# One 1.5 MB fetch per weight chunk in place of a 1 MB and a 0.5 MB fetch, in a two-layer decoder trunk

## The chip, the cores and the metric

The kernel runs on one core of a Trainium2 chip. The metric is the device time in microseconds; lower is better. Five engines work beside each other: TensorE (PE; its weight loads are PEld), VectorE (DVE), ScalarE (ACT), GpSimd (POOL) and SyncE (SP), which here issues nearly all DMAs. Each engine works through its own instructions in order, and they wait for each other on semaphores.

## The reference, cut to what matters

Two layers, each an FFN, a mixing block and a second FFN, on 256 tokens of width 1024 in float32:

```python
for l in range(DEPTH):            # DEPTH = 2
    h = h + 0.5 * swiglu(rms_norm(h, ffn1_norm[l]), ffn1_gate[l], ffn1_up[l], ffn1_down[l])
    h = h + token_mixing(rms_norm(h, mix_norm[l]), w_in[l], ...)   # top-k sparse attention beside a forgetting attention
    h = h + 0.5 * swiglu(rms_norm(h, ffn2_norm[l]), ffn2_gate[l], ffn2_up[l], ffn2_down[l])
return rms_norm(h, final_norm)
```

`swiglu` has an inner width of 2816, which is 22 tiles of 128.

## The kernel before, in words

**The weight stream.** The host lays all weights out as 112 chunks (`stream`), 56 to a layer: 22 for the first FFN, 12 for the mixing block, 22 for the second FFN. A chunk is 128 partitions by 3072 floats, 1.5 MB. Its first 2048 columns are its front (an FFN chunk's gate and up weights), the last 1024 its back (the down weights). `raw` holds two chunks, chunk c in slot c % 2.

**The split.** Every float32 weight is split into a high and a low float32r part, so that the product is near float32. ACT copies `raw` to `whi` (front: two casts of 1024 columns, line 370; back: one, line 374), then DVE writes `wlo = raw - whi` (lines 1065 and 1071). In the mixing block POOL does this subtraction for the chunks m = 4 and the front of m = 5 (lines 306, 315). When both low halves of a front are written, semaphore `w_front` has counted 2 more; when the low back is, `w_back` has counted 1 more. Then that part of the slot in `raw` is free.

**The fetches.** SP's program is a plain order of waits and transfers. `reload(i)` fetches the chunks 2i and 2i+1: for each it waits until the front of the chunk two before is split, issues the front's 1 MB (line 246), waits until that chunk's back is split, and issues the back's 0.5 MB (line 250):

```python
def reload(i):
    for s in range(2):
        sp.wait_ge(w_front, (i * 2 + s - 1) * 2)
        load_front(s, i)
        sp.wait_ge(w_back, i * 2 + s - 1)
        load_back(s, i)
```

Between `reload(2)` and `reload(3)` SP also issues a copy within DRAM (`table<-table`, line 270), which builds the relative bias, and after `reload(3)`, once that copy is done, the fetches of `bias` and `fgain` (lines 275, 276). All of them go to the same DMA queue.

**An FFN step.** PE runs up(f), down(f-1), up(f+1), down(f), and so on, a step being one up and one down. In step f, ACT and DVE first make the hidden values of tile f (lines 408 to 415 on ACT, 1140 to 1161 on DVE), then split the back of chunk f+1, then the front of chunk f+2. So of one chunk the front is split a step before its back.

**The mixing block.** The orders of ACT, DVE, POOL and PE are written out by hand. What matters here is the part around the chunks m = 3 to 6. DVE runs the top-k rounds (`take`, lines 1201 and 1204) with `tile_sum(t)` (line 1247) and splits set between them. `tile_sum(t)` waits for ACT's `tile_low(t)` (line 503). ACT's order there is front(5), tile_low(3), back(5), tile_low(4), tile_low(5), front(6). After the last round DVE writes `drop` (line 1324), for which PE's first logits (line 821) wait; later DVE's `turned(0)` (line 1229) frees the bank into which PE's `turn(1)` (line 839) writes. Front(5) is the front of chunk 27 (layer 0) and of chunk 83 (layer 1). Its fetch can go, as far as buffers are concerned, once chunk 25 (81), m = 3, is split; the back of m = 3 is split late, by DVE between two top-k rounds.

Of the kernel before, what the change touches and what calls it, by code (L numbers as in the profile page):

```python
# [45 lines left out]
FRONT = 2 * UNIT  # L46
CHUNK = 3 * UNIT
# [36 lines left out]
def trunk(nc, x, stream, gains, final_gain, consts, rel_bias, out, table):  # L84
    with ExitStack() as ctx:
        def sb(name, shape, dt=F32):
            return ctx.enter_context(nc.sbuf_tensor(name, shape, dt))

        def sems(names):
            return [ctx.enter_context(nc.semaphore(n)) for n in names.split()]  # L90


        raw = sb("raw", [P, 2, CHUNK])
# [96 lines left out]

        front_in, back_in = sems("front_in0 front_in1"), sems("back_in0 back_in1")
        lead_in, x_in = sems("lead_in0 lead_in1"), sems("x_in0 x_in1")
        lead_hi, id_in = sems("lead_hi id_in")
        table_in, const_in, rb_in, gain_in, fgain_in = sems("table_in const_in rb_in gain_in fgain_in")
# [30 lines left out]
        def arrivals(l, k, i=0):  # L227

            return (l * (LC // 2) + i + (k // 2 + 1)) * 16

        def front_arrivals(l, k, i=0):

            return arrivals(l, k, i) if k % 2 else (l * (LC // 2) + i + k // 2) * 16
# [4 lines left out]
        @block.sync  # L238
        def _(sp):
            sp.dma_start(X[:, 0, :], x[:, 0, :]).then_inc(x_in[0], 16)  # L240
            sp.dma_start(X[:, 1, :], x[:, 1, :]).then_inc(x_in[1], 16)
            for g in range(2):
                sp.dma_start(raw[:, 0, g * UNIT:(g + 1) * UNIT], stream[0, :, g * UNIT:(g + 1) * UNIT]).then_inc(lead_in[g], 16)

            def load_front(s, i):
                sp.dma_start(raw[:, s, 0:FRONT], stream[bass.ds(i * 2 + s, 1), :, 0:FRONT].rearrange(
                    "a p n -> (a p) n")).then_inc(front_in[s], 16)

            def load_back(s, i):
                sp.dma_start(raw[:, s, FRONT:CHUNK], stream[bass.ds(i * 2 + s, 1), :, FRONT:CHUNK].rearrange(  # L250
                    "a p n -> (a p) n")).then_inc(back_in[s], 16)

            def reload(i):
                for s in range(2):
                    sp.wait_ge(w_front, (i * 2 + s - 1) * 2)
                    load_front(s, i)
                    sp.wait_ge(w_back, i * 2 + s - 1)
                    load_back(s, i)

            load_front(1, 0)  # L260
            load_back(0, 0)
            load_back(1, 0)
            sp.dma_start(cst[:, C_CM:NC], consts[:, C_CM:NC]).then_inc(const_in, 16)
            reload(1)

            sp.wait_ge(tab_sb, 1)
            sp.dma_start(table[:, 0:TAB], tab).then_inc(table_out, 16)
            reload(2)
            sp.wait_ge(table_out, 16)
            sp.dma_start(table[:, TAB:P * TAB].rearrange("h (p y) -> h p y", y=TAB),  # L270
                         table[:, 0:TAB].unsqueeze(1).to_broadcast([NH, P - 1, TAB])).then_inc(table_out, 16)
            reload(3)
            sp.wait_ge(table_out, 32)
            skew = table[:, P - 1:P - 1 + P * (TAB - 1)].rearrange("h (p y) -> p h y", y=TAB - 1)
            sp.dma_start(bias[:, :, :], skew[:, :, 0:S]).then_inc(bias_in, 16)
            sp.dma_start(fgain[:, :], final_gain).then_inc(fgain_in, 16)
            with sp.Fori(4, NCHUNK // 2) as i:
                reload(i)
            for b in range(NB):
                for j in range(2):  # L280
                    at = slice(j * 512, (j + 1) * 512)
                    sp.wait_ge(fin_out, 2 * b + j + 1)
                    sp.dma_start(out[b, :, at], xn[:, b, at]).then_inc(out_done, 16)
            sp.wait_ge(out_done, 16 * NB * 2)
# [80 lines left out]
        def _(act):  # L365
            def split_front(l, k, i=0, used=FRONT):

                act.wait_ge(front_in[k % 2], front_arrivals(l, k, i))
                for at in (slice(0, used // 2), slice(used // 2, used)):
                    nc.scalar.copy(whi[:, k % 2, at], raw[:, k % 2, at]).then_inc(hi_front, 1)  # L370

            def split_back(l, k, i=0, used=UNIT):
                act.wait_ge(back_in[k % 2], arrivals(l, k, i))
                nc.scalar.copy(whi[:, k % 2, FRONT:FRONT + used],  # L374
                               raw[:, k % 2, FRONT:FRONT + used]).then_inc(hi_back, 1)

# [5 lines left out]
            def norm(n, g, l, first=False):  # L382


                squares(n, 0)
                for k in range(KT):
                    if k % 2 == 0:
                        act.wait_ge(xt_mm, n * (KT // 2) + (k // 2 + 1))
                    nc.scalar.mul(xhi[:, k, :], ps[:, 4 + k // 2, S * (k % 2):S * (k % 2) + S],
                                  gains_all[:, l, g + k:g + k + 1]).then_inc(xhi_out, 1)  # L390
                if first:
                    act.wait_ge(lead_in[1], 16)
                    nc.scalar.copy(whi[:, 0, UNIT:FRONT], raw[:, 0, UNIT:FRONT]).then_inc(hi_front, 2)
                squares(n, 1)
                if first:
                    split_front(l, 1)

            def ffn(l, phase):
                k0 = phase * (NF + MIXC)

                def step(f, i=0, back=UNIT, front=FRONT):


                    s, n = f % 2, l * (2 * NF) + i * 2 + (phase * NF + f)
                    bank = GU + 2 * s
                    if f > 0:
                        act.wait_ge(gate_mm, n + 1)
                        nc.scalar.copy(glo[:, s, :], ps[:, bank, S:2 * S]).then_inc(glo_out, 1)
                    act.wait_ge(hg_out, n + 1)
                    nc.scalar.activation(sig[:, s, :], hg[:, s, :], ACT.Sigmoid).then_inc(sig_out, 1)  # L410
                    if 0 < f < NF - 1:
                        act.wait_ge(front_done, n + 1)
                        nc.scalar.copy(ulo[:, s, :], ps[:, bank + 1, S:2 * S]).then_inc(ulo_out, 1)
                    act.wait_ge(h_out, n + 1)
                    nc.scalar.copy(hhi[:, s, :], hf[:, s, :]).then_inc(hhi_out, 1)  # L415
                    if back:
                        if f > 0:
                            act.wait_ge(back_done, n)
                        split_back(l, k0 + f + 1, i, back)
                    if front:  # L420
                        act.wait_ge(front_done, n + 1)
                        split_front(l, k0 + f + 2, i, front)
# [14 lines left out]
            def mix(l):  # L437
                def front(m):
                    split_front(l, NF + m, used=MIX_USED[m][0] if m < MIXC else FRONT)

                def back(m):
                    split_back(l, NF + m, used=MIX_USED[m][1] if m < MIXC else UNIT)
# [140 lines left out]
            for l in range(DEPTH):  # L583
                norm(l * 3, G_FFN1, l, first=l == 0)
                if l == 0:
                    split_back(l, 0)
                ffn(l, 0)
                norm(l * 3 + 1, G_MIX, l)
                mix(l)
                norm(l * 3 + 2, G_FFN2, l)  # L590
                ffn(l, 1)
# [913 lines left out]
```

## Time and profile before

| | |
|---|---|
| median of 3 runs | 1011.92 us (1011.25 to 1012.65) |
| the profiled execution | 1012.57 us, of which its span, from the first to the last instruction, is 1010.7 us |
| granted TensorE clock, mean | 0.997 |
| PE busy | 997.6 us, 99% of the span |
| DVE busy | 763.0 us, 75% |
| ACT busy | 538.5 us, 53% |
| POOL busy | 124.7 us, 12% |
| DMA | 183.17 MB, 181 GB/s over the span; the main queue took 54.6% of the 16 engines' time |

The chain of work that ended last is 93% PE, 3% DVE, 2% DMA and 1% ACT. Matmuls are pipelined, so their durations overlap.

In the timelines a row gives the start in microseconds, the duration in microseconds, the engine, the line, the operation and its tiles; in brackets stands how long the engine was idle before it, and what ended that.

### The profile page before, as it was taken

To read this page: it belongs to the slowest core of one execution; us is meant where nothing else is said; L and a number is where in the kernel's file an instruction comes from. 1 tells how busy PE (TensorE), PEld (TensorE's weight loads), DVE (VectorE), ACT (ScalarE), POOL (GpSimd) and SP (SyncE) were. 2 spreads that over 40 slices of the span, in tenths; PEclk is the share of its full clock that TensorE was granted. 3 is DMA by queue.
4 is the path that set the end of the run, shared out by engine and by line. 5 is a ranking of instruction groups with operands and counts; after the bars stand their busy time and mean duration, and the time that the engine had idled before them with its cause. 6 is when DMAs were issued, how large, how long until landed. Compare 5 with 4: busy or idle time off the path is not lost.

```text
span 1010.7 us, 16529 instructions
## 1 busy us (share of the span) xinstructions
PE 997.6 (99%) x5652; PEld 846.2 (84%) x5652; DVE 763.0 (75%) x1556; ACT 538.5 (53%) x974; POOL 124.7 (12%) x148
## 2 busy tenths in 40 slices
PE   9999999999999999999999999999999999999996
PEld 8878888898878888888888888889887788888885
DVE  6868777688677877777788777777786778777775
ACT  5545555566556555555555555555755555555552
POOL 1000000018552000000000000000185400000000
PEclk9999999999999999999999999999999999999998
DMA  8786556544525665555536555554363446555541
GB/s 319 223 277 208 190 185 189 184 160 137 205 68 182 194 221 187 186 187 187 188 126 211 187 188 188 187 187 149 137 213 121 164 152 219 194 187 187 187 145 42
DMA packets 36053, 183.17 MB, mean 181 GB/s; under 512 B 3984, under 2 KB 6192, under 8 KB 21680
## 3 DMA queue, kind: packets, MB, share of 16 engines
q1 hardware_dynamic: 35632, 182.53, 54.6%
q8 instruction: 23, 0.38, 0.2%
q10 hardware_dynamic: 384, 0.15, 0.1%
q14 instruction: 14, 0.11, 0.0%
HBM read 181.61 MB, written 2.62 MB: 182 GB/s over the span
## 4 chain that ended last, share of the span: by engine, by line
PE 93%; DVE 3%; DMA 2%; ACT 1%; issue 1%; POOL 0%; POOLq 0%; DVEq 0%; SPq 0%; ACTq 0%
PE ps L606 31%; PE ps L607 16%; PE ps L600 12%; PE ps L602 12%; PE ps L601 12%; DMA raw<-stream 2%; PE ps L839 1%; PE ps L616 1%; DVE wlo L1065 1%; PE ps L674 1%; PE ps L620 1%; PE ps L617 1%; PE ps L851 1%; PE ps L830 1%; PE ps L826 1%
## 5 line engine op out<-in xcount | busy, mean ns | idle before, releaser
L606 PE MATMUL ps<-xboth,whi 128*128 128x512 f32 x1440 | 508.5, 395 | 1.5 <-DVE wlo L1065 1.5
L607 PE MATMUL ps<-xboth,wlo 128*128 128x256 f32 x1440 | 403.1, 280 | 0.0
L606 PEld LDWEIGHTS ps<-xboth,whi 128*128 128x128 f32 x1440 | 270.0, 188 | 66.0 <-DVE wlo L1065 2.1
L607 PEld LDWEIGHTS ps<-xboth,wlo 128*128 128x128 f32 x1440 | 271.9, 189 | 3.3
L1065 DVE TENSOR_TENSOR wlo<-raw,whi 128x1024 fp32r<-128x1024 f32 (+2 forms) x215 | 251.0, 1204 | 9.3 <-ACT whi L370 9.3
L370 ACT CAST whi<-raw 128x1024 fp32r<-128x1024 f32 (+1 forms) x222 | 217.5, 1029 | 14.6 <-PE ps L602 9.2
L1071 DVE TENSOR_TENSOR wlo<-raw,whi 128x1024 fp32r<-128x1024 f32 (+1 forms) x110 | 131.9, 1199 | 99.6 <-ACT whi L374 99.5
L410 ACT ACTIVATE sig<-hg 128x256 f32<-128x256 f32 x88 | 36.8, 418 | 198.6 <-DVE hg L1142 182.2
L374 ACT CAST whi<-raw 128x1024 fp32r<-128x1024 f32 (+1 forms) x112 | 112.7, 1006 | 51.7 <-PE ps L602 51.5
L600 PE MATMUL ps<-whi,hhi 128*128 128x512 f32 x352 | 139.2, 395 | 0.0
L602 PE MATMUL ps<-whi,hlo 128*128 128x512 f32 x352 | 139.1, 395 | 0.0
L601 PE MATMUL ps<-wlo,hhi 128*128 128x512 f32 x352 | 138.5, 394 | 0.0
L297 POOL TENSOR_TENSOR rstd<-ms,mhalf 128x1 f32<-128x1 f32 x14 | 13.5, 976 | 776.9 <-DVE ms L1082 776.9
L415 ACT CAST hhi<-hf 128x256 fp32r<-128x256 f32 x88 | 35.8, 406 | 97.7 <-DVE hf L1159 97.7
L602 PEld LDWEIGHTS ps<-whi,hlo 128*128 128x128 f32 x352 | 66.1, 188 | 16.1
L600 PEld LDWEIGHTS ps<-whi,hhi 128*128 128x128 f32 x352 | 66.1, 188 | 15.7
L601 PEld LDWEIGHTS ps<-wlo,hhi 128*128 128x128 f32 x352 | 66.1, 188 | 12.5
L1161 DVE TENSOR_TENSOR hlo<-hf,hhi 128x256 fp32r<-128x256 f32 x88 | 37.4, 425 | 41.6 <-ACT hhi L415 41.6
L600 PE MATMUL ps<-xboth,whi 128*128 128x256 f32 x160 | 46.4, 290 | 0.0
L601 PE MATMUL ps<-xboth,whi 128*128 128x256 f32 x160 | 45.2, 282 | 0.0
L602 PE MATMUL ps<-xboth,wlo 128*128 128x256 f32 x160 | 45.2, 282 | 0.0
L1147 DVE TENSOR_TENSOR ht<-ur,sig 128x256 f32<-128x256 f32 x88 | 37.5, 426 | 9.2
(172 smaller groups left out, 1189.6 us busy)
## 6 DMA issues: line engine op xcount, KB each, us to landing
raw<-stream SPq DMA_DIRECT2D x111, 1024.0 KB, 5.2
raw<-stream SPq DMA_DIRECT2D x114, 512.0 KB, 3.6
table<-table SPq DMA_DIRECT2D x1, 1524.0 KB
cst<-consts SPq DMA_DIRECT2D x1, 1088.0 KB, 12.8
X<-x SPq DMA_DIRECT2D x2, 512.0 KB, 5.1
bias<-table SPq DMA_DIRECT2D x1, 1024.0 KB, 10.3
out<-feat SPq DMA_DIRECT2D x4, 256.0 KB, 2.0
fgain<-final_gain SPq DMA_DIRECT2D x1, 512.0 KB, 11.2
```

The lines of the kernel that those rows point to most:

```text
L370: nc.scalar.copy(whi[:, k % 2, at], raw[:, k % 2, at]).then_inc(hi_front, 1)
L374: nc.scalar.copy(whi[:, k % 2, FRONT:FRONT + used], raw[:, k % 2, FRONT:FRONT + used]).then_inc(hi_back, 1)
L410: nc.scalar.activation(sig[:, s, :], hg[:, s, :], ACT.Sigmoid).then_inc(sig_out, 1)
L600: nc.tensor.matmul(out_, a[0], b[0], start=start, stop=False)
L601: nc.tensor.matmul(out_, a[0], b[1], start=False, stop=False)
L602: return nc.tensor.matmul(out_, a[1], b[0], start=False, stop=stop)
L606: nc.tensor.matmul(ps[:, bank, :], a[0], xboth[:, k, :], start=k == 0, stop=False)
L607: return nc.tensor.matmul(ps[:, bank, 0:S], a[1], xhi[:, k, :], start=False, stop=k == KT - 1)
L1065: nc.vector.tensor_tensor(wlo[:, s, at], raw[:, s, at], whi[:, s, at].bitcast(F32), ALU.subtract).then_inc(w_front, 1)
L1071: nc.vector.tensor_tensor(wlo[:, s, at], raw[:, s, at], whi[:, s, at].bitcast(F32), ALU.subtract).then_inc(w_back, 1)
L1147: nc.vector.tensor_tensor(ht[:, s, :], ur[:, s, :], sig[:, s, :], ALU.mult).then_inc(ht_out, 1)
L1161: nc.vector.tensor_tensor(hlo[:, s, :], hf[:, s, :], hhi[:, s, :].bitcast(F32), ALU.subtract).then_inc(hlo_out, 1)
```

## The change

The front and the back of a chunk are fetched by one transfer, and it is issued once both parts of the chunk two before are split. The back of chunk 0 keeps a transfer of its own, which now comes behind the whole of chunk 1. ACT's waits follow: both the front's and the back's split of a chunk wait for its one transfer.

```diff
-        front_in, back_in = sems("front_in0 front_in1"), sems("back_in0 back_in1")
+        chunk_in, tail_in = sems("chunk_in0 chunk_in1"), sems("tail_in")[0]
...
-            def load_front(s, i):
-                sp.dma_start(raw[:, s, 0:FRONT], stream[bass.ds(i * 2 + s, 1), :, 0:FRONT].rearrange(
-                    "a p n -> (a p) n")).then_inc(front_in[s], 16)
-
-            def load_back(s, i):
-                sp.dma_start(raw[:, s, FRONT:CHUNK], stream[bass.ds(i * 2 + s, 1), :, FRONT:CHUNK].rearrange(
-                    "a p n -> (a p) n")).then_inc(back_in[s], 16)
+            def load(s, i):
+                sp.dma_start(raw[:, s, :], stream[bass.ds(i * 2 + s, 1), :, :].rearrange(
+                    "a p n -> (a p) n")).then_inc(chunk_in[s], 16)
 
             def reload(i):
                 for s in range(2):
                     sp.wait_ge(w_front, (i * 2 + s - 1) * 2)
-                    load_front(s, i)
                     sp.wait_ge(w_back, i * 2 + s - 1)
-                    load_back(s, i)
-
-            load_front(1, 0)
-            load_back(0, 0)
-            load_back(1, 0)
+                    load(s, i)
+
+            sp.dma_start(raw[:, 1, :], stream[1, :, :]).then_inc(chunk_in[1], 16)
+            sp.dma_start(raw[:, 0, FRONT:CHUNK], stream[0, :, FRONT:CHUNK]).then_inc(tail_in, 16)
...
             def split_front(l, k, i=0, used=FRONT):
 
-                act.wait_ge(front_in[k % 2], front_arrivals(l, k, i))
+                act.wait_ge(chunk_in[k % 2], front_arrivals(l, k, i))
...
             def split_back(l, k, i=0, used=UNIT):
-                act.wait_ge(back_in[k % 2], arrivals(l, k, i))
+                if (l, k) == (0, 0):
+                    act.wait_ge(tail_in, 16)
+                else:
+                    act.wait_ge(chunk_in[k % 2], front_arrivals(l, k, i))
```

## Rows read from the trace of the kernel before

**Rows 1.** The page's part 1, busy time by engine.

```profile
PE 997.6 (99%) x5652; PEld 846.2 (84%) x5652; DVE 763.0 (75%) x1556; ACT 538.5 (53%) x974; POOL 124.7 (12%) x148
```

**Rows 2.** What PE waited for, whole span: us in total, times, longest.

```profile
PE ps L606 <- DVE wlo L1065: 1.5, 1, 1.5
```

**Rows 3.** Fetches of fronts (line 246), issue to landing, from 66 us on.

```profile
L246 SPq DMA_DIRECT2D raw<-stream x103: 332/333/333, 70.1 to 971.2; - x103
...
DMA to landing us min/median/max: 4.7/5.2/7.0
```

**Rows 4.** Fetches of backs (line 250), issue to landing, from 66 us on.

```profile
DMA to landing us min/median/max: 3.3/3.6/7.1
```

**Rows 5.** Timeline of SP's queue in a middle step of the first FFN.

```profile
164.89 0.33 SPq L250 DMA_DIRECT2D raw<-stream  x1
...
173.23 0.33 SPq L250 DMA_DIRECT2D raw<-stream  x1
```

**Rows 6.** Timeline of ACT in the same step.

```profile
170.77 1.05 ACT L374 CAST whi<-raw 128x1024 fp32r<-128x1024 f32 x1 [0.75 <-PE ps L602]
171.72 2.00 ACT L370 CAST whi<-raw 128x1024 fp32r<-128x1024 f32 x2
```

**Rows 7.** Timeline of DVE, the split of a front in the next step.

```profile
181.44 2.35 DVE L1065 TENSOR_TENSOR wlo<-raw,whi 128x1024 fp32r<-128x1024 f32 x2
```

**Rows 8.** Timeline of PE, the first matmul that reads that front.

```profile
187.28 0.40 PE L606 MATMUL ps<-xboth,whi 128*128 128x512 f32 x1
```

**Rows 9.** Timeline of ACT at the start.

```profile
17.21 0.48 ACT L426 ACTIVATE prT<-ps 8x384 f32<-8x384 f32 x1 [1.12 <-PE ps L652]
...
23.43 1.99 ACT L370 CAST whi<-raw 128x1024 fp32r<-128x1024 f32 x2
```

**Rows 10.** Timeline of SP's queue at the start: the back of chunk 2.

```profile
19.86 0.33 SPq L250 DMA_DIRECT2D raw<-stream  x1
```

**Rows 11.** Timeline of PE, the first matmul on chunk 2.

```profile
26.05 0.42 PE L606 MATMUL ps<-xboth,whi 128*128 128x512 f32 x1
```

**Rows 12.** Timeline of SP's queue around the copy within DRAM.

```profile
40.18 0.73 SPq L270 DMA_DIRECT2D table<-table  x1
...
47.31 0.33 SPq L250 DMA_DIRECT2D raw<-stream  x1
```

**Rows 13.** The fetch of 47.31 us (back of chunk 6) alone, issue to landing.

```profile
DMA to landing us min/median/max: 12.9/12.9/12.9
```

**Rows 14.** Timelines of ACT and PE, chunk 6.

```profile
58.97 1.99 ACT L370 CAST whi<-raw 128x1024 fp32r<-128x1024 f32 x2 [5.44 <-DMA raw<-stream]
...
61.33 0.49 PE L606 MATMUL ps<-xboth,whi 128*128 128x512 f32 x1 [1.51 <-DVE wlo L1065]
```

**Rows 15.** Timeline of SP's queue: the backs of chunks 27 and 83.

```profile
236.61 0.33 SPq L250 DMA_DIRECT2D raw<-stream  x1
...
732.82 0.33 SPq L250 DMA_DIRECT2D raw<-stream  x1
```

**Rows 16.** Timeline of ACT: the fronts of chunks 27 and 83.

```profile
236.99 2.00 ACT L370 CAST whi<-raw 128x1024 fp32r<-128x1024 f32 x2
...
733.19 2.00 ACT L370 CAST whi<-raw 128x1024 fp32r<-128x1024 f32 x2
```

**Rows 17.** Timeline of DVE in the mixing block: tile_sum(3), tile_sum(5), drop, turned(0).

```profile
240.03 0.42 DVE L1247 TENSOR_TENSOR val<-ps,ht 128x256 f32<-128x256 f32 x1 [0.43 <-ACT ht L503]
...
245.75 0.42 DVE L1247 TENSOR_TENSOR val<-ps,ur 128x256 f32<-128x256 f32 x1 [1.15 <-ACT ur L503]
...
247.46 0.87 DVE L1324 SCALAR_TENSOR_TENSOR drop<-score,cst 128x384 bf16<-128x384 f32 x1
...
263.43 0.55 DVE L1229 COPY prT<-ps 128x384 f32<-128x384 f32 x1
```

**Rows 18.** Timeline of PE in the mixing block: first logits, turn(1).

```profile
250.74 0.50 PE L821 MATMUL ps<-drop,nident 128*128 128x384 bf16 x2
...
265.33 0.38 PE L839 MATMUL ps<-cst,pr 128*128 128x128 f32 x2
```

**Rows 19.** Engines and clock by stretch: busy us and instructions of PE, PEld, DVE, ACT, POOL; clock; DMA.

```profile
1005.50:1010.50 5.00, 0.00 (x0) 0.00 (x0) 2.27 (x5) 0.00 (x0) 0.99 (x1) 0.50 0.55 210
```

## The prediction

> **What bounds the kernel now.** I read the busy times first: PE is busy for 997.6 of 1010.7 us [rows 1]. Then what PE waited for: for the split of an FFN front it waited once in the whole span, 1.5 us at 61 us [rows 2, 14]. So the kernel is bound by PE, and a change to the fetches can gain next to nothing; what it can do is make PE wait. The question is therefore where the fetched data comes late by more than the work queued ahead of PE covers. I looked for that in the timelines of SP's queue and ACT: for every chunk, the time between the moment at which its back may be fetched (now also its front's moment) and the moment at which ACT starts to cast its front.
>
> **What the change does.** It removes one of two issues per chunk on SP, 0.33 us each, on an engine that mostly waits: nothing. It moves the fetch of each front from "front of c-2 split" to "back of c-2 split", and it makes the front wait for 1.5 MB instead of 1 MB. The backs are issued when they were, and needed a step later than they land: nothing. SP's new wait stands where its old second wait stood; what is queued behind it are the next chunk's fetch and, early on, the copy within DRAM.
>
> **The price of 1.5 MB.** No such transfer is in the trace. A front's 1 MB lands 5.2 us after issue in the median and 4.7 at best [rows 3], a back's 0.5 MB 3.6 and 3.3 [rows 4]. The step from 0.5 to 1 MB costs 1.4 to 1.6 us, so 1.5 MB costs 6.1 (minima) to 6.8 (medians). Part of the front's median is a back still in flight, which falls away; I take L = 6.4. Bounds: 5.2, if size were free from here on, and 7.0 + 1.6 = 8.6 from the slowest front. ACT starts some 0.1 us after a landing.
>
> By the Trainium skill, page "DMA: Bandwidth & Descriptors", section "Anatomy of one DMA", a transfer issued by GpSimd costs 2.0 us plus its bytes at 436 GB/s. For 1.5 MB that would be an estimate of 5.6 us, and the delays summed below would be 7.4 us instead of 9.8. For 1 MB it gives 4.4 us where this trace has 5.2, so the rows decide.
>
> **Steady FFN steps: covered.** A back's split releases the fetch at 164.89 [rows 5]; ACT wants that slot's front at 171.72 [rows 6]: 6.8 us for L = 6.4 plus 0.1. If L is longer, ACT has 0.75 us of idle time before each back's cast [rows 6] before later steps move, and PE has more: its first half of a front is written at about 181.44 + 1.2 = 182.6 [rows 7] and read at 187.28 [rows 8], 4.6 us later. Early in a phase ACT and DVE still catch up with PE, whose step is 8.34 us [rows 5]; they will catch up more slowly, and PE is not reached. Cost 0.
>
> **The start: 2.7 us.** Chunk 1 as one piece lands about 1.3 us later than its front alone did; ACT's cast moves by half a microsecond and is covered by its idle 1.12 us at 17.21 [rows 9]. Chunk 2 is another matter. Its fetch now goes at 19.86 [rows 10] and lands at 26.3, while ACT started at 23.43 [rows 9]. From ACT's start to PE's first matmul are 2.36 us, by the same pair for chunk 6, 58.97 to 61.33 [rows 14]. So PE starts chunk 2 at 26.3 + 0.1 + 2.3 = 28.7 instead of 26.05 [rows 11]: 2.7 us late, without any cover.
>
> **The copy within DRAM: 1.3 us more.** ACT and DVE run this stretch back to back, so SP reaches the copy at 40.18 [rows 12] 2.7 us late too, and whatever is queued behind the copy moves by that. Before, the front of chunk 6 landed behind it at 58.9 (ACT starts at 58.97 [rows 14]) and the back at 47.31 + 12.86 = 60.2 [rows 12, 13]. One transfer lands when the back did: 1.3 us later than the front. Chunk 6's front is what PE waits for [rows 14]. Here PE is 2.7 + 1.3 = 4.0 us late; the old 1.5 us stall becomes about 2.9.
>
> **The mixing block: 2.9 us in each layer.** The back of m = 3 is split late, so the fetch of chunk 27 goes at 236.61 [rows 15], and ACT starts its front at 236.99 [rows 16]. It lands at 243.0, ACT starts at 243.1: 6.1 us late. Queued behind on ACT is tile_low(3), for which DVE waits inside its top-k sequence: tile_sum(3) goes from 240.03 to 243.1 + 2.0 + 0.3 = 245.4, 5.35 us late. DVE then runs without a break, and gets back the 1.15 us for which it had waited before tile_sum(5) [rows 17]: 4.2 us late. `drop` is written at 248.33 + 4.2 = 252.5, where PE wanted it at 250.74 [rows 18]: 1.8 us. PE then waits further, as DVE stays 4.2 us late while PE has 1.35 us in hand at turn(1) (turned(0) ends at 263.98 [rows 17], turn(1) starts at 265.33 [rows 18]): in all 4.2 - 1.35 = 2.85 us. Behind that the two meet again. POOL's subtraction for front(5) starts after other work of POOL's, so it loses less than ACT does; I take it as not last. The next fetch, m = 6, falls into the same delay. Layer 1 has the same gap, 732.82 to 733.19 [rows 15, 16]. Bounds for a layer: 0, if the delay is covered by something that I read as waiting, and 4.2, if PE has nothing in hand. Sum 5.7. The front of m = 11 will be cast late as well, but the casts and the subtraction behind it are wanted later than that.
>
> **The sum** is 4.0 + 5.7 = 9.7, say 9.8 us. The profiled execution took 1012.57 us with a span of 1010.7, so one like it would take 1022.4; it lies 0.65 above the median, so against 1011.92 I predict **1021.7 us**. Each microsecond of L moves the sum by 3.
>
> **Rivals.**
> - *The mixing block is covered.* If DVE has more room than I read between tile_sum(3) and turned(0), only the start remains: 1011.92 + 4.0 = 1015.9. For it: PE has hardly any stall there now, so its reserve is not visible in waits. Against: drop is only 2.4 us ahead of PE. 12%.
> - *The clock falls in the new stalls.* PE would stand still for about 2.7 and 2.9 us in the start. The granted clock is 1.0 throughout the stall of 1.5 us, but 0.50 (the 1.2 GHz level) in the tail where PE has stopped [rows 19]. At that level a step of 8.34 us takes up to 8.3 us more; taking a third of that after each of two stalls gives 5.6 more: 1027.3. The Trainium skill, page "TensorE: Matmul & The Clock Gate", section "Why this matters for your kernels", warns of just such idle gaps between bursts. 8%.
> - *The steady steps become bound by landing.* From L = 6.8 + 0.75 = 7.6 on, each second step is late by the excess. At 8.6 that is 0.5 us in each of some 80 steps, less the 4.6 us in hand in each of four phases: about 20 us, 1042. Only the slowest fronts point there. 3%.
> - *Not slower.* If a 1.5 MB transfer landed as fast as a back's 0.5 MB (3.6 us) since latency were nearly all of it, chunk 2 would be there at 23.5, the mixing block's 3.2 us would be covered, and chunk 6 could gain at most the 1.5 us stall: 1010.4 to 1011.9. It decides at L below about 4. The 1.6 us between 0.5 and 1 MB speaks against it. 3%.
> - *The change does not do what it says*, for instance if the transfer were cut in two again behind the issue: then landing would still be that of 1.5 MB, and the time that of the forecast; 1% for no difference at all.
>
> **The numbers.** The forecast holds 73%. Its own range is L from 6.1 to 7.2 (-0.9 to +2.4) and the mixing block between 2.0 and 4.2 us a layer (-1.7 to +2.7): 1019 to 1026. With the first rival taken in, and part of the second, the range is 1015.8 to 1027.0. About 0.2%, 2 us, is what a measurement of this kernel can tell from no change. Faster 1%, same 3%, slower 96%.
>
> **What would show it.** In the changed profile: median landing of the one fetch 6.4 us; ACT's cast of chunk 2 ended by DMA, near 26.3; PE waits for line 1065 of about 2.7 and 2.9 us at 28.7 and 65; ACT's cast of front(5) ended by DMA with some 6 us of idle time; PE waiting for `drop` (1.8 us) and for line 1229 in both layers; no DMA wait of ACT over half a microsecond in the middle of an FFN. It is wrong if ACT waits for DMA in each FFN step and PE behind it, if PE has no wait at line 821, or if the clock row shows less than 1.00 anywhere before the tail.

## The result and the profile after

The changed kernel takes **1027.24 us** in the median of 4 runs (1026.03 to 1029.44), the kernel before 1011.59 (1010.81 to 1012.65): a ratio of 1.0157, 95% interval 1.014 to 1.0174. It is 15.65 us slower, where 9.8 were forecast. The median lies 0.24 us above the predicted range, which is less than the scatter of the four runs, but 5.5 us above the predicted time. The profiled execution took 1027.48 us, its span is 1025.6 us against 1010.7: 14.9 us more, and the place-by-place account below divides these 14.9. One of the eleven executions of an experiment's kernel (nine chunks in two parts) took 2522.87 us, for no reason that the record shows, and its ratio leaves it out.

What PE waited for, the seven largest entries (line, what ended it, us in total, times, longest):

```profile
PE ps L603 <- DVE wlo L1062: 5.4, 2, 2.9
PE ps L818 <- DVE drop L1321: 2.2, 2, 1.1
PE ps L1043 <- DVE nc L1380: 1.5, 1, 1.5
PE ps L848 <- DVE prT L1226: 1.3, 2, 0.7
PE ps L613 <- ACT xboth L386: 1.0, 2, 0.6
PE ps L597 <- DVE feat L1236: 0.7, 1, 0.7
PE ps L836 <- DVE prT L1226: 0.7, 2, 0.4
...
```

Line 603 here is line 606 before [rows 2]: one wait of 1.5 us has become two, 5.4 us together. The waits at 818 (`drop`) and 836 (`turn(1)`) are new and stand where the prediction put them. The one at 597, for a feature tile between these two, was not named, and those at 613, in front of a norm's first product, were not forecast. The waits at 1043 and 848 were there before.

The fetches from 70 us on, issue to landing (min, median, max), the counterpart of [rows 3]:

```profile
L246 SPq DMA_DIRECT2D raw<-stream x104: 332/333/351, 73.4 to 992.4; - x104
...
DMA to landing us min/median/max: 6.0/6.3/9.1
```

The median of 6.3 us agrees with the 6.4 forecast. The slowest, 9.1 us, is above the slowest of before (7.0 for a front, 7.1 for a back [rows 3, 4]).

SP's queue at the start and around the copy within DRAM. A row with "x2" merges two issues: the first at its start, the second at its end.

```profile
19.95 5.28 SPq L246 DMA_DIRECT2D raw<-stream  x2
25.28 0.37 SPq L261 DMA_DIRECT2D table<-prT  x1
35.23 7.83 SPq L246 DMA_DIRECT2D raw<-stream  x2
43.11 0.74 SPq L264 DMA_DIRECT2D table<-table  x1
50.24 8.31 SPq L246 DMA_DIRECT2D raw<-stream  x2
60.49 0.38 SPq L269 DMA_DIRECT2D bias<-table  x1
```

Chunk 2 is fetched at 19.95 as forecast. The copy is issued 2.9 us later than before [rows 12]. `bias` waits for the copy, so its issue at 60.49 tells when the copy was done: 17.4 us after its issue. Before, these were 16.3 us. SP's rows of before, the front of chunk 7, its back, and `bias`:

```profile
49.58 0.33 SPq L246 DMA_DIRECT2D raw<-stream  x1
54.81 0.33 SPq L250 DMA_DIRECT2D raw<-stream  x1
56.44 0.39 SPq L275 DMA_DIRECT2D bias<-table  x1
```

ACT, the casts that waited for chunks 2, 6 and 27:

```profile
26.49 1.04 ACT L364 CAST whi<-raw 128x1024 fp32r<-128x1024 f32 x1 [2.93 <-DMA raw<-stream]
...
64.56 1.99 ACT L364 CAST whi<-raw 128x1024 fp32r<-128x1024 f32 x2 [7.68 <-DMA raw<-stream]
...
251.08 2.00 ACT L364 CAST whi<-raw 128x1024 fp32r<-128x1024 f32 x2 [5.68 <-DMA raw<-stream]
```

PE: the first matmul on chunk 2, on chunk 6, on the later front of [rows 8], the first logits of both layers, and the norm's product in both layers:

```profile
28.85 0.80 PE L603 MATMUL ps<-xboth,whi 128*128 128x512 f32 x1 [2.59 <-DVE wlo L1062]
...
66.92 0.80 PE L603 MATMUL ps<-xboth,whi 128*128 128x512 f32 x1 [2.85 <-DVE wlo L1062]
...
195.58 0.40 PE L603 MATMUL ps<-xboth,whi 128*128 128x512 f32 x1
...
260.10 0.50 PE L818 MATMUL ps<-drop,nident 128*128 128x384 bf16 x2 [1.14 <-DVE drop L1321]
...
332.99 0.36 PE L613 MATMUL ps<-xboth,whi 128*128 128x256 f32 x1 [0.41 <-ACT xboth L386]
...
709.06 0.35 PE L613 MATMUL ps<-xboth,whi 128*128 128x256 f32 x1 [0.63 <-ACT xboth L386]
...
760.55 0.50 PE L818 MATMUL ps<-drop,nident 128*128 128x384 bf16 x2 [1.08 <-DVE drop L1321]
```

The same matmul in both traces tells how far PE is behind:

| PE's matmul | before, us | changed, us | behind |
|---|---|---|---|
| first on chunk 2 | 26.05 | 28.85 | 2.8 |
| first on chunk 6 | 61.33 | 66.92 | 5.6 |
| on the later front of [rows 8] | 187.28 | 195.58 | 8.3 |
| turn(1), layer 0 | 265.33 | 276.43 | 11.1 |
| the norm behind it | 321.31 | 332.99 | 11.7 |
| the norm ahead of layer 1's mixing block | 696.68 | 709.06 | 12.4 |
| turn(1), layer 1 | 761.27 | 776.09 | 14.8 |

At the end of the span it is 14.9. So the start costs 8.3 us and everything behind it 6.6: 2.8 and 2.5 in the two mixing blocks, 0.5 and 0.7 at two norms. Between chunk 6 and 195 us PE waits for nothing, yet loses 2.7 us. The stretches show where (busy us and instructions of PE, PEld, DVE, ACT, POOL; clock; DMA):

```profile
28.90:31.80 2.90, 2.90 (x9) 2.52 (x10) 2.73 (x6) 0.68 (x2) 0.00 (x0) 0.50 0.60 250
...
66.10:72.80 6.70, 5.88 (x18) 5.01 (x19) 5.50 (x10) 3.59 (x7) 0.00 (x0) 0.50 0.51 186
73.00:80.00 7.00, 7.00 (x38) 5.95 (x37) 5.79 (x11) 3.45 (x7) 0.00 (x0) 1.00 0.60 225
```

Behind each of the two stalls the granted clock is 0.50, the 1.2 GHz level, and behind the second PE gets through 18 matmuls in 6.7 us instead of 38 in 7. This was the second rival, and it came on top of the forecast.

### The profile page after: what moved, and what is told of

It is laid out like the page before. It is cut to its first block, busy times and chain, and to the rows that moved or that the text cites. A ratio compares the mean times of both kernels' runs of the same rounds, so it can differ in the third digit from the quotient of the medians.

```text
span 1025.6 us, 16320 instructions
## 1 busy us (share of the span) xinstructions
PE 1003.3 (98%) x5652; PEld 849.4 (83%) x5652; DVE 761.7 (74%) x1556; ACT 539.8 (53%) x974; POOL 120.4 (12%) x148
## 4 chain that ended last, share of the span: by engine, by line
PE 81%; DMA 7%; DVE 6%; ACT 3%; issue 2%; POOL 0%; SPq 0%; POOLq 0%; DVEq 0%; ACTq 0%
PE ps L603 28%; PE ps L604 14%; PE ps L597 11%; PE ps L599 10%; PE ps L598 10%; DMA raw<-stream 7%; ACT whi L364 2%; DVE wlo L1068 1%; DVE wlo L1062 1%; PE ps L613 1%; PE ps L836 1%; PE ps L617 1%; PE ps L614 1%; PE ps L848 1%; ACT whi L371 1%
```

## Experiments

The question was how the 14.9 us divide among four suspects: the late chunk 2, the copy within DRAM, the clock, and the mixing block; and whether the 1.5 MB transfers cost anything in the steady FFN steps. They were timed in four groups, each beside the kernel before, whose medians were 1011.72, 1011.62, 1011.55 and 1011.36 us.

**The clock.** Extra matmuls on constant data, into the bank that PE is about to overwrite anyway, just before PE's wait for a chunk, 14 ahead of chunk 2 and 16 ahead of chunk 6; a second kernel has only those ahead of chunk 6. To single these chunks out, the first turns of PE's loop are written out:

```diff
+                        if g == 0 and isinstance(i, int):
+                            for _ in range({2: 14, 6: 16}.get(chunk(l, k0 + f, i), 0)):
+                                nc.tensor.matmul(ps[:, GU + 2 * s, 0:S3], nc2[:, 0:P], nc2[:, :], start=True, stop=True)
                         front_here(l, k0 + f, i, g)
...
-                with pe.Fori(0, NF // 2 - 2) as i:
+                peel = 3 if (l, phase) == (0, 0) else 0
+                for i in range(peel):
...
+                with pe.Fori(peel, NF // 2 - 2) as i:
```

> The changed kernel, with 14 and 16 extra matmuls that PE runs before it waits for chunk 2 and for chunk 6, so that it works through most of the two stalls (2.6 and 2.9 us). Clock theory: both falls of the clock go, the one at 66 us is worth 2.7 us at the end, the one at 28 us nothing, because the wait for chunk 6 takes up whatever was lost before it: about 1024.5 against 1027.2. Rival (the loss is in the late data alone, the clock costs nothing): 1027 or more.

Measured: 1024.54 us (ratio to the kernel before 1.0133, 1.0118 to 1.0147).

> The changed kernel with the 16 extra matmuls before chunk 6 alone. If the fall of the clock at 28 us is hidden in the wait for chunk 6, this is as fast as with extra matmuls at both places, about 1024.5. Rival (each fall costs by itself): about 1.5 us slower than that.

Measured: 1022.58 us (1.011, 1.0094 to 1.0125). Stretches of this kernel behind chunk 2's stall and behind chunk 6, its first matmul on chunk 6, and the later one of the table:

```profile
30.10:33.30 3.20, 3.20 (x12) 2.72 (x11) 2.52 (x7) 1.49 (x4) 0.00 (x0) 0.50 0.14 59
66.10:72.80 6.70, 6.70 (x40) 5.98 (x39) 5.50 (x10) 3.82 (x6) 0.00 (x0) 1.00 0.55 201
```

```profile
66.81 0.39 PE L603 MATMUL ps<-xboth,whi 128*128 128x512 f32 x1
...
192.66 0.40 PE L603 MATMUL ps<-xboth,whi 128*128 128x512 f32 x1
```

PE begins chunk 6 at 66.81, practically as late as in the changed kernel, but now at full clock, with 40 matmuls (a few of them extra ones) in the stretch that had 18. Behind that its lag does not grow: 5.5 us at chunk 6, 192.66 - 187.28 = 5.4 later. So the fall at 66 us was worth the 2.7 us. The fall behind chunk 2 is still there (0.50), and costs next to nothing, since chunk 6 is waited for anyway: without that fall, with extra matmuls at both places, PE starts chunk 6 at 66.46.

The time is another matter. This kernel came out 1.9 us below the 1024.5 expected: layer 0's mixing block costs it 1.7 us by lag (272.42 - 265.33 = 7.1 behind, less 5.4) in place of 2.8, and PE waits at no norm; the record does not show why. The kernel with extra matmuls at both places met the 1024.5, but partly by luck: it lost 2 us more in layer 1's mixing block. The question was whether that loss is chance:

> The same kernel as in the first run with extra matmuls. It was 2 us slower than the one with extra matmuls before chunk 6 alone, and its profile has that in the second layer's mixing block (a wait of 2.3 us for drop and a short fall of the clock behind it). If that is chance in the landings, 1022.5 to 1024.5 and no fall of the clock before the tail in the profile; if the extra matmuls at chunk 2 cause it, again 1024.5 with the fall.

Measured: 1024.20 us (1.0129, 1.0113 to 1.0144), the same once more. In its second layer PE waits longer for `drop`, because DVE waited longer for tile_low(3); their rows:

```profile
756.27 0.34 PE L827 MATMUL ps<-drop,nident 128*128 128x384 bf16 x1 [2.15 <-DVE drop L1330]
```

```profile
749.55 0.42 DVE L1253 TENSOR_TENSOR val<-ps,ht 128x256 f32<-128x256 f32 x1 [6.46 <-ACT ht L500]
```

In the changed kernel these waits are 1.08 and 5.7 us. Chunk 83 landed 7.1 us after issue there, 7.5 in the first run of the same kernel, and the clock falls behind the longer stall in both. In the changed kernel and in the one with extra matmuls before chunk 6 alone it landed after 6.3 and 6.2. All eight executions of the slower kernel took 1023.44 us or more, all four of the other 1023.11 or less, so it is hardly chance. The traces show one difference at that place. In the first 5 us of that fetch, both slow cases have a 16 KB packet of the queue that the profile's page calls `q8 instruction`:

```profile
q8 instruction: 1, 0.02, 1.9%
```

The two others have none there. That this packet delays the fetch was not tested.

**Chunk 2 alone in two parts.** The helper with which the following kernels were made; a chunk in `TWO` is fetched in two parts at the old moments:

```diff
+                    if c in TWO:
+                        sp.dma_start(raw[:, s, 0:FRONT], stream[c, :, 0:FRONT]).then_inc(chunk_in[s], 16)
                     sp.wait_ge(w_back, i * 2 + s - 1)
+                    if c in TWO:
+                        sp.dma_start(raw[:, s, FRONT:CHUNK], stream[c, :, FRONT:CHUNK]).then_inc(tail_in[s], 16)
+                    else:
                         load(s, i)
```

> The changed kernel with chunk 2 alone fetched in two parts as before. No wait at chunk 2 then. Theory of the queue: the copy within DRAM still starts behind all of chunk 5, and chunk 6 lands whole, so PE's wait for chunk 6 grows to about 4.2 us, the clock falls once, and some 5.4 of the 8.3 us lost by then remain: about 1024.3. Rival (all of the start's loss comes from chunk 2's delay): the loss goes down to 1.3 us, about 1020.

Measured: 1022.52 us (1.0108, 1.0093 to 1.0122), between the two, a little nearer the queue's theory. The first entry of what PE waited for in it:

```profile
PE ps L616 <- DVE wlo L1075: 3.8, 1, 3.8
```

The wait at chunk 2 is gone and the one at chunk 6 has grown to 3.8 us. Taking chunk 2's delay away saves 4.7 us of 15.65: the start's loss is not its alone.

**What lies around the copy within DRAM.** First four and five chunks in two parts:

> The changed kernel with chunks 2, 5, 6, 27 and 83 in two parts, the 106 others in one transfer. If the loss sits in these five places, this is as fast as the kernel before to within 1 us: 1011.6 to 1012.6. Rival (1.5 MB transfers cost a little in each FFN step): it stays above 1015.

Measured: 1012.81 us (1.0015, 1.0005 to 1.0026). Five chunks of 111 carry nearly all of the loss; 1.1 us is left. Two of its eleven executions took 1016.57 and 1016.67 us; they were not profiled, and what they waited for is not known.

> As the run with five chunks in two parts, but chunk 5 whole again: only what lies in the queue ahead of the copy within DRAM differs. Theory of the queue: the copy starts 1 MB later, chunk 6's front lands about 1.4 us later than in the kernel before, PE's wait of 1.5 us becomes 2.9, and the clock falls for 2.7 us more: about 1015.7. Rival (only the time of issue of the copy matters): no difference from the run with five, about 1012.

Measured: 1015.45 us (1.0041, 1.0027 to 1.0054), close to the 1015.7 expected. But its profiled execution, with 1014.04 us the fastest of the five, shows a shorter wait for chunk 6 than the 2.9 us expected, and no fall of the clock:

```profile
61.20 0.50 PE L626 MATMUL ps<-xboth,whi 128*128 128x512 f32 x1 [1.33 <-DVE wlo L1085]
```

So the number agrees, and the way to it is not seen in this trace. Nor were these two kernels timed side by side, so the question was put again as a square, `TWO` being 2, 23, 27, 35, 79, 83 and 91, with and without 5 and 6:

> One corner of a square: chunks 2, 23, 27, 35, 79, 83 and 91 in two parts throughout, and here 5 and 6 as well. As before (the kernel of the run with nine): within 0.5 us of the kernel before, the copy within DRAM done some 15.5 us after its issue.

> The same with chunk 5 in one transfer, 6 in two parts. Theory (the copy waits in the queue behind what is left of chunk 5): the copy is done 1 to 1.5 us later after its issue, PE reads chunk 6 that much later, 1 to 2 us slower than the corner with both in two parts, more where the clock falls. Rival (what is ahead of the copy does not matter, only chunk 6 behind it does): no difference.

> The same with chunk 5 in two parts, 6 in one transfer. Theory of the prediction: chunk 6 lands whole, 1.3 us later than its front alone: 1.3 us slower than the corner with both in two parts, more where the clock falls. Rival (chunk 6's front, issued right behind the copy, had been served in part beside it, and the whole chunk comes too late for that): over 2 us slower.

> The same with both in one transfer. If the two add up, the wait for chunk 6 is 1.5 + 1.3 + 1.3 = 4.1 us at the most, less what the corner with both in two parts gains on the kernel before; with one fall of the clock of 1.5 to 2.7 us some 4 to 6 us slower than that corner, near 1016 to 1017.

| | chunk 6 in two parts | chunk 6 whole |
|---|---|---|
| chunk 5 in two parts | 1011.47 us, 1.0000 (0.9991 to 1.0009) | 1012.01 us, 1.0006 (0.9997 to 1.0015) |
| chunk 5 whole | 1014.28 us, 1.0027 (1.0018 to 1.0036) | 1016.96 us, 1.0051 (1.0037 to 1.0065) |

PE's first matmul on chunk 6: chunk 5 whole, then chunk 6 whole, then both. In the fourth corner there is no wait at all.

```profile
61.83 0.50 PE L638 MATMUL ps<-xboth,whi 128*128 128x512 f32 x1 [2.09 <-DVE wlo L1097]
```

```profile
61.04 0.50 PE L638 MATMUL ps<-xboth,whi 128*128 128x512 f32 x1 [1.30 <-DVE wlo L1097]
```

```profile
63.40 0.79 PE L634 MATMUL ps<-xboth,whi 128*128 128x512 f32 x1 [3.64 <-DVE wlo L1093]
```

Chunk 5 whole costs 2.8 us by itself, chunk 6 whole 0.5, both 5.5. The 0.5 is within the scatter of the medians, and less than the 1.3 expected; the wait of 1.30 us in its profile is as expected. The waits add up: 2.09 + 1.30 = 3.4 against 3.64. The times add up to more. In the profiles, the clock fell behind the stall of 2.09 us and not behind that of 1.30, and behind 3.64 it was down about twice as long as behind 2.09:

```profile
62.40:65.70 3.30, 3.30 (x12) 2.82 (x11) 2.88 (x7) 0.85 (x3) 0.00 (x0) 0.50 0.94 337
65.80:69.50 3.70, 3.70 (x22) 3.24 (x21) 3.01 (x4) 3.24 (x5) 0.00 (x0) 1.00 0.32 77
...
62.80:69.50 6.70, 6.10 (x19) 5.22 (x20) 5.50 (x10) 3.59 (x8) 0.00 (x0) 0.50 0.49 180
```

So the queue's theory held for what is *ahead* of the copy: 1.5 MB of chunk 5, issued just before it, hold it up more than 0.5 MB did. The other profiles agree: with chunk 5 whole, 16.0 to 17.4 us pass from the copy's issue to `bias`; with chunk 5 in two parts and chunk 7 whole, at most 15.5. What is *behind* it, the only thing that the prediction had counted, is the smaller term of this square.

The fourth corner has no wait, although the kernel before, which also fetches chunks 5 and 6 in two parts, has one of 1.51 us. SP's rows of this corner, chunk 7 and `bias`:

```profile
54.85 0.33 SPq L252 DMA_DIRECT2D raw<-stream  x1
55.23 0.43 SPq L281 DMA_DIRECT2D bias<-table  x1
```

The copy, issued at 40.10, was done within 15.1 us, where the kernel before took 16.3. Chunk 7's front, which goes out at 49.58 beside the copy in the kernel before, here waits until 54.85. That this makes the difference fits the rows but was not tested by itself; chunks 3 and 4 are whole here too.

**The mixing block.**

> The changed kernel with chunks 27 and 83, the fronts of m = 5 in the two mixing blocks, fetched in two parts as before. Theory of the prediction: PE's waits for drop, for the feature tiles and at turn(1) go, 2.9 us a layer: about 1021.4, or 1020.6 if all of the 6.6 us lost behind the start is due to them. Rival (late landings in general): less than 2 us gained.

Measured: 1020.73 us (1.0087, 1.0074 to 1.0099), 6.5 us less than the changed kernel. The waits for `drop` and at turn(1) are gone from the list. This is not the price of the two mixing blocks alone. The waits for `xboth` at the norms are absent from this profile too, and in layer 1 there is a new one:

```profile
756.31 0.36 PE L616 MATMUL ps<-xboth,whi 128*128 128x256 f32 x1 [0.88 <-DVE val L1263]
```

By PE's lag, the profile of the changed kernel puts the two places at 2.8 and 2.5 us.

**The waits at the norms.** What was left with five chunks in two parts was PE waiting for `xboth`, 0.7 us in two waits. Here chunks 23, 35, 79 and 91 are in two parts too:

> As the run with five chunks in two parts, with chunks 23, 35, 79 and 91 in two parts too. Their fronts stand before a norm's work in ACT's queue. Theory: the late landings there (up to 8 us) are what made PE wait for xboth at a norm, 0.4 to 0.8 us at a time; with them in two parts no wait of PE for xboth is left, and the time is that of the kernel before to within 0.5 us. Rival (those waits come from elsewhere, or other chunks land as late): no change from the run with five, about 1 us above the kernel before.

Measured: 1011.43 us (1.0002, 0.9992 to 1.0011), and no wait for `xboth` in the list. With nine chunks in two parts and 102 in one the kernel is as fast as before, to within 1.1 us. It also has no wait for chunk 6, so the equality of the times alone could hide a small loss elsewhere. The changed kernel's table settles it: from 332.99 to 709.06, with two FFNs between them, the lag grows by 0.7 us, and PE's wait at the second norm is 0.63 of that. The steady FFN steps pay nothing for the 1.5 MB transfers, which was the prediction's zero.

**Later issue or larger piece?** The kernel before with only its two waits moved together:

```diff
                     sp.wait_ge(w_front, (i * 2 + s - 1) * 2)
+                    sp.wait_ge(w_back, i * 2 + s - 1)
                     load_front(s, i)
-                    sp.wait_ge(w_back, i * 2 + s - 1)
                     load_back(s, i)
```

> The kernel before with both waits ahead of both fetches: each front is issued as late as in the changed kernel, but as its own 1 MB, with the 0.5 MB right behind it. Tells the later issue from the larger piece. Theory: a front now lands 5.2 us after issue, not 6.4. Start: 1.5 us at chunk 2; the copy within DRAM still starts behind 1.5 MB, so 1.5 + 1.6 = 3.1 at chunk 6, and the clock falls there for 2.7; mixing block 1.65 us a layer: about 1020.7. Rival (the size of the piece makes the loss, not the moment of issue): within 2 us of the kernel before.

Measured: 1017.28 us (1.0051, 1.0037 to 1.0065), 3.4 us better than expected. PE's waits for fronts fall to 1.11 and 2.23 us, and the mixing block is nearly free:

```profile
27.42 0.50 PE L606 MATMUL ps<-xboth,whi 128*128 128x512 f32 x1 [1.11 <-DVE wlo L1065]
...
63.51 0.50 PE L606 MATMUL ps<-xboth,whi 128*128 128x512 f32 x1 [2.23 <-DVE wlo L1065]
...
191.07 0.40 PE L606 MATMUL ps<-xboth,whi 128*128 128x512 f32 x1
```

So of 15.65 us some 5.7 come from issuing the front later, and the other 10 from the front having to wait for the back's bytes as well. By lag, the start costs 191.07 - 187.28 = 3.8 us here and 8.3 in the changed kernel, so 4.5 of the 10 lie in the start. The size counts for more than 1.2 us a place, because it takes the delays over what covers them. The clock falls here too, behind the stall of 2.23 us, but behind that alone and for less time than in the changed kernel:

```profile
64.90:68.10 3.20, 3.20 (x11) 2.72 (x10) 2.49 (x7) 1.57 (x4) 0.00 (x0) 0.50 0.80 283
68.30:70.00 1.70, 1.70 (x12) 1.49 (x11) 1.41 (x2) 1.70 (x3) 0.00 (x0) 1.00 0.14 55
```

**The copy in pieces.** In both kernels the copy within DRAM was cut into 8, one piece behind the fetch of each of the chunks 4 to 11, so that `bias` and `fgain` are fetched later too:

```diff
-            reload(2)
             sp.wait_ge(table_out, 16)
-            sp.dma_start(table[:, TAB:P * TAB].rearrange("h (p y) -> h p y", y=TAB),
-                         table[:, 0:TAB].unsqueeze(1).to_broadcast([NH, P - 1, TAB])).then_inc(table_out, 16)
-            reload(3)
-            sp.wait_ge(table_out, 32)
+            def piece(a, n):
+                sp.dma_start(table[:, a * TAB:(a + n) * TAB].rearrange("h (p y) -> h p y", y=TAB),
+                             table[:, 0:TAB].unsqueeze(1).to_broadcast([NH, n, TAB])).then_inc(table_out, 16)
+            for i in range(2, 6):
+                reload(i, lambda s: piece(1 + 16 * ((i - 2) * 2 + s), 15 if (i, s) == (5, 1) else 16))
+            sp.wait_ge(table_out, 16 * 9)
...
```

> The changed kernel with the copy within DRAM cut into 8 pieces, one behind the fetch of each of the chunks 4 to 11. The wait for chunk 6 goes; what is left of the start is chunk 2's 2.7 us and 1.5 us for the clock's fall behind it: 4.2 + 6.6 behind 1011.6, about 1022.4. Rival (each piece delays a fetch that has no slack): PE waits in several of the steps 4 to 11, above 1025.

Measured: 1021.44 us (1.0101, 1.0086 to 1.0117), a microsecond better than expected: the wait for chunk 6 is gone, the one for chunk 2 stays.

> The kernel before with the copy within DRAM cut into the same 8 pieces. Its one wait of 1.5 us for chunk 6 goes: about 1010.1 against 1011.6. Rival (the copy's 1.5 us is taken back elsewhere): no difference.

Measured: 1011.03 us (0.9994, 0.9985 to 1.0003), and once more:

> The kernel before with the copy within DRAM in 8 pieces, once more, to narrow the interval: 0.6 to 1.7 us faster than the kernel before.

Measured: 1010.75 us (0.9991, 0.9982 to 1.0000). The wait for chunk 6 is gone from both profiles. The gain is 0.6 and 0.8 us, less than the wait's 1.5, and at the edge of what can be told. The profiled execution of the kernel before lies 1.0 us above the median of its four, so its wait may be longer than the usual one; that is not shown. It is the only version that may beat both kernels.

## Why the prediction was wrong, step by step

The failed part of the prediction is its sum: the copy's term was put at 1.3 us and measured 2.8; the clock, kept out of the sum as a rival, took 2.7; the norms, not in it at all, took 1.2. The largest of these is the clock. The other terms held.

**What bounds the kernel, and where it would hurt: right.** The loss sits at chunk 2, around the copy, and at m = 5 of both layers; taken back there, all but 1.1 us of it is gone.

**L = 6.4 us: right** (6.3). So was the choice of the rows over the page's formula: by the Trainium skill, page "DMA: Bandwidth & Descriptors", section "Anatomy of one DMA", the estimate had been 5.6 us.

**Steady steps at 0: right.** ACT waits for DMA in several steps, 0.2 to 1.1 us at a time, where the prediction had none over half a microsecond, and PE for a front in none.

**Chunk 2, 2.7 us: right.** PE is 2.8 us late there.

**The copy, 1.3 us: mis-sized; measured 2.8** (5.6 at chunk 6, less 2.8). The step that failed is "SP reaches the copy 2.7 us late too, and whatever is queued behind the copy moves by that". The copy was issued 2.9 us late but was done 4.05 us late (60.49 against 56.44): it took 1.1 us longer itself (one execution each). ACT's cast of chunk 6 came 5.6 us late (64.56 against 58.97 [rows 14]), 1.5 more than the copy, where the prediction had 1.3 for that. I had looked at what stands behind the copy in the queue and not at what stands ahead of it, although the change triples what SP issues just before it. The square shows that what stands ahead matters: chunk 5 whole makes PE wait 2.09 us, where chunk 6 whole makes it wait 1.30.

**The clock: a rival at 8%, and it happened.** The prediction had named the two stalls (2.7 and 2.9 us; measured 2.59 and 2.85) and then gave the fall of the clock after them a small chance, although stalls of that length were its own forecast and the only evidence to the contrary was a stall half as long. Its price, 2.8 us for each stall, was right for the second (2.7). For the first it should have been next to nothing: chunk 6 arrives at its own time, and PE, 66.92 us with both falls and 66.46 with neither, waits for it either way. The Trainium skill, page "TensorE: Matmul & The Clock Gate", section "Why this matters for your kernels", warned of idle gaps of PE between bursts of matmuls; the trace agrees, with 0.50 behind gaps of 2.59 and 2.85 us.

**The mixing block, 2.9 us a layer: right in size,** 2.8 and 2.5 by PE's lag. Its waits at `drop` and turn(1) are where they were worked out. Those for `drop` are shorter, 1.14 and 1.08 us where 1.8 was forecast, with one for a feature tile beside them in layer 0. It is one execution's value: the kernel with extra matmuls before chunk 6 alone lost 1.7 in layer 0.

**The norms: not in the sum; measured 0.5 and 0.7.** The fronts ahead of a norm had a reserve against a landing of 6.4 us. These two landed after 7.9 and 7.5. The prediction took one value of L for all 111 transfers where the tail of their distribution was what met the places with little reserve. Its range for L, 6.1 to 7.2 us, ended below these two.

The sum with these corrections: 2.8 + 2.8 + 2.7 + 2.8 + 2.5 + 1.2 = 14.8 of the profile's 14.9 us. That is 5 us above the 9.8 forecast, since all three missing terms (1.5 of the copy's, the clock and the norms) lay on the same side. That the median ended just outside the range and not just inside is chance: one of the four executions, 1026.03 us, lies inside.

## What to carry to other kernels

When a transfer is made larger or later, look at what the queue carries behind it *and* at what it now holds up: with 1 MB more issued just ahead of it, the copy within DRAM took 1.1 us longer here, and the chunk that PE waits for was behind it. When a forecast contains a stall of TensorE longer than any in the trace, give the lower clock after it a price in the sum, except where a later wait for DMA takes the loss up again. And a change that is harmless in 102 of 111 cases can be confined to them: fetching whole only where a full step lies between issue and use costs nothing that these runs can tell, but here it gains nothing either.

## What the runs showed of the hardware that I had not expected

- Stalls of PE of 1.51 us and less left the granted clock at 1.00. Each of those from 2.09 us on (2.09, 2.15, 2.23, 2.32, 2.43, 2.59, 2.61, 2.85, 3.40, 3.64 and 3.82 in the profiles) had a stretch at 0.50 at its end or just behind it, but for one: behind chunk 2 in the kernel with 27 and 83 in two parts, 2.75 us without a fall. So the length of a stall does not settle it alone. Nor does it settle for how long the clock is down. Behind 3.82 us, with chunk 2 alone in two parts, that was about as short as behind 2.09:

```profile
63.90:67.20 3.30, 3.30 (x11) 2.81 (x11) 3.09 (x7) 0.68 (x2) 0.00 (x0) 0.50 0.71 257
67.40:70.70 3.30, 3.30 (x21) 2.88 (x20) 2.37 (x3) 3.30 (x5) 0.00 (x0) 1.00 0.08 32
```

- The copy within DRAM took from its issue to `bias` 16.3 us in the kernel before and 17.4 in the changed one, with the same bytes. Kernels that fetch the chunks around it alike still differ: 16.0 and 16.7 with chunk 5 whole and chunk 6 in two parts. So of the 1.1 us between the two a part may be scatter between executions.
- From 70 us on, a 1.5 MB transfer lands between 6.0 and 9.1 us after issue, while in the kernel before no separate part took over 7.1 there. Beside the copy within DRAM all are slower: chunk 6 took 14.3 us whole. Places with 0.5 us in reserve see this tail.
- The tail has a pattern. Of the 104 transfers seven took over 7.0 us. The two slowest, 9.1 and 8.7 us, were issued at 265.2 and 765.6, while the chunk before was still in flight (issued at 261.4 and 761.9, landed after 7.4 and 6.6). Each of the other five, those ahead of the norms among them, had a packet of `q8 instruction` during its flight. So had some that landed after 6.3 to 6.5 us, and no run tests it.
